# Gate matrices of a PEER layer from split operands: one 256-column product per token instead of one 128-column fp32 product

## The reference

```
q = (xb @ wq).reshape(PEER_TOKEN_BLOCK, PEER_HEADS, 2, PEER_HALF_DIM)
s = jnp.einsum('thpd,hpnd->thpn', q, keys).astype(jnp.float32)
s1, i1 = lax.top_k(s[:, :, 0], PEER_TOPK)
s2, i2 = lax.top_k(s[:, :, 1], PEER_TOPK)
...
top_s, pos = lax.top_k(cand_s, PEER_TOPK)
idx = jnp.take_along_axis(cand_i, pos, axis=-1)
gate = jax.nn.softmax(top_s, axis=-1)
act = jax.nn.gelu(jnp.einsum('thkd,td->thk', u[idx], xb).astype(jnp.float32), approximate=False)
return jnp.einsum('thk,thkd->td', (gate * act).astype(xb.dtype), v[idx])
```

## Time and profile before

| | us |
|---|---|
| median of the runs | 3306.17 |
| the profiled execution's own time | 3303.77 |
| its span | 3302.0 |
| PE busy | 3233.7 (98%) |
| DVE busy | 2537.3 (77%) |
| POOL busy | 2078.6 (63%) |
| ACT busy | 1409.5 (43%) |
| gate products on PE (1536 instructions), busy | 202.7 |

### The profile page before, as it was taken

The page is one execution under the profiler, slowest core; times in us unless marked ns, Lnnn a source line. Parts: engine busy times, 40 slices in busy tenths (PEclk is TensorE's granted clock), DMA queues, the critical chain, the costliest instruction groups (busy, mean ns, idle before and its releaser), DMA issues. The chain is left out here.

```text
span 3302.0 us, 47513 instructions
## 1 busy us (share of the span) xinstructions
PE 3233.7 (98%) x17562; PEld 2882.6 (87%) x17562; DVE 2537.3 (77%) x4630; ACT 1409.5 (43%) x2756; POOL 2078.6 (63%) x1388
## 2 busy tenths in 40 slices
PE   8999999999999999999999999999999999999998
PEld 6787789999999988888787877899999999888886
DVE  8964469876966688888877734798769656988888
ACT  2244113566666433333322531245666664333332
POOL 7913776666677655555499047766666776555553
PEclk9999999999999999999999999999999999999999
DMA  4211326688899999999622012257888999999995
GB/s 150 89 46 39 103 77 201 230 305 297 298 344 353 353 389 372 364 369 363 244 90 90 33 52 92 94 202 255 300 298 298 349 353 352 386 373 365 369 366 197
DMA packets 312918, 817.11 MB, mean 247 GB/s; under 512 B 22512, under 2 KB 119792, under 8 KB 309360
## 3 DMA queue, kind: packets, MB, share of 16 engines
q1 hardware_dynamic: 112496, 348.98, 30.7%
q0 software_dynamic: 73728, 268.47, 20.9%
q10 hardware_dynamic: 126464, 196.63, 17.0%
HBM read 712.79 MB, written 101.19 MB: 247 GB/s over the span
## 5 line engine op out<-in xcount | busy, mean ns | idle before, releaser
L1323 POOL TENSOR_TENSOR u_lo<-panel,u_hi 128x1024 fp32r<-128x1024 f32 x256 | 619.4, 2420 | 317.6 <-ACT u_hi L1122 314.4
L605 PE MATMUL ps<-hT_hi,u_lo 128*128 128x384 f32 x2048 | 700.3, 342 | 0.0
L605 PE MATMUL ps<-hT_lo,u_hi 128*128 128x384 f32 x2048 | 684.6, 334 | 0.0
L605 PE MATMUL ps<-hT_hi,u_hi 128*128 128x384 f32 x2048 | 684.6, 334 | 0.0
L605 PE MATMUL ps<-v_hi,w_lo 128*128 128x512 f32 x1536 | 598.0, 389 | 3.0 <-DVE w_lo L1907 2.9
L605 PE MATMUL ps<-v_hi,w_hi 128*128 128x512 f32 x1536 | 597.6, 389 | 0.0
L605 PE MATMUL ps<-v_lo,w_hi 128*128 128x512 f32 x1536 | 597.5, 389 | 0.0
L1340 POOL TENSOR_TENSOR v_lo<-panel,v_hi 128x1024 fp32r<-128x1024 f32 x128 | 312.8, 2444 | 370.6 <-ACT v_hi L1184 370.5
L1184 ACT CAST v_hi<-panel 128x1024 fp32r<-128x1024 f32 x256 | 269.0, 1052 | 633.0 <-PE ps L605 626.5
L1273 POOL TENSOR_TENSOR ring_hi<-panel,cst 128x512 fp32r<-128x512 f32 x244 | 283.7, 1163 | 359.4 <-PE ps L585 250.8
L1122 ACT CAST u_hi<-panel 128x1024 fp32r<-128x1024 f32 x256 | 268.1, 1048 | 446.5 <-PE ps L605 435.4
(11 more groups left out here) (272 smaller groups left out, 5695.1 us busy)
## 6 DMA issues: line engine op xcount, KB each, us to landing
panel<-in_u SPq DMA_DIRECT2D x256, 512.0 KB
panel<-in_v SPq DMA_DIRECT2D x256, 512.0 KB
gate_scratch<-arena ACTq DMA_DIRECT2D x24, 2048.0 KB
act_scratch<-arena ACTq DMA_DIRECT2D x124, 384.0 KB
arena<-act_scratch ACTq DMA_DIRECT2D x62, 768.0 KB
arena<-gate_scratch ACTq DMA_DIRECT2D x62, 768.0 KB
panel<-in_w_in SPq DMA_DIRECT2D x28, 1024.0 KB, 5.2
panel<-in_wq SPq DMA_DIRECT2D x16, 1024.0 KB, 5.1
```

The costliest lines, as they stand in the source:

```text
L605: mm = nc.tensor.matmul(o, lhs[a], rhs[b_], start=(start and n == 0), stop=(stop and n == 2))
L1323: pr.mark(nc.gpsimd.tensor_tensor(u_lo[:, j % URING].rearrange("p c n -> p (c n)"), u_tile(j), u_hi[:, j % URING].rearrange("p c n -> p (c ...
```

## The change

The gate products are done with operands of fp32r instead of fp32. The one-hots are exact in any format; the gates are split into a high part (rounded to fp32r) and a low part (the rest). For each token hot2 (now bf16) is weighed twice, by the high and by the low gate, into two halves of a 256-column operand `gated`. One matmul of hot1 by these 256 columns gives two 128x128 halves in PSUM, which are added on the way out: ACT copies the first half to `gmat` (`keep_half`), and DVE adds the second to it (`keep_gates`, now on DVE). Four tokens now take two PSUM banks, so the product of chunk k+1 waits until the sum of k is out (`g_kept` of k, before: of k-1), and there is one buffer of `gated`. DVE's `keep_gates(k-2)` stands at the head of its gate chunk k. Every 32 chunks DVE makes the high and low gates with two instructions of 128x128. The DMA of a finished block goes one chunk later, the transposes of the table go into the middle of the chunk, ACT's copy of them ahead of its wait for the chunk, and DOTS is spread anew: two dots in three chunks where the routing lies, five in four chunks from 20 to 45.

```diff
-    DOTS.append(min(DOTS[-1] + 1 + (chunk_ >= 58 and chunk_ % 2 == 0), SLOTS - LATE_DOTS))
+    routed_beside = chunk_ < 20 or 46 <= chunk_ < 60
+    DOTS.append(min(DOTS[-1] + 1 + (chunk_ >= 60 and chunk_ % 2 == 0) + (20 <= chunk_ < 46 and chunk_ % 4 == 3)
+                    - (routed_beside and chunk_ % 3 == 2), SLOTS - LATE_DOTS))
...
+            hot1 = half("hot1", 2 * CHUNK * NK)[:].rearrange("p (b c k) -> p b c k", b=2, c=CHUNK)
+            gated = half("gated", 2 * CHUNK * NK)[:].rearrange("p (c r k) -> p c r k", c=CHUNK, r=2)
...
+        hot2 = sb("hot2", [P, 2, CHUNK, NK], BF16)
...
+        chunk_banks = ps[:, GBANKS[0]:GBANKS[1] + 1, :].rearrange("p b (c r n) -> p (b c) r n", c=2, r=2)
...  (PE)
                     for c in range(NC):
+                        if j in TURNS and c == NC // 2:
+                            i = TURNS[j]
+                            pe.wait_ge(table_ready.sem, layer * table_ready.per_layer + i)
+                            if j > FIRST_CHUNK:
+                                pe.wait_ge(g_kept.sem, layer * g_kept.per_layer + j - FIRST_CHUNK)
...
-                        if k >= 2:
-                            pe.wait_ge(g_kept.sem, layer * g_kept.per_layer + k - 1)
+                        if k >= 1:
+                            pe.wait_ge(g_kept.sem, layer * g_kept.per_layer + k)
...
                         for c in range(CHUNK):
-                            mm = nc.tensor.matmul(g_bank(k)[:, c * NK:(c + 1) * NK],
-                                                  hot1[:, k % 2, c, :], hot2[:, k % 2, c, :], start=True, stop=True)
+                            mm = nc.tensor.matmul(chunk_banks[:, c].rearrange("p r n -> p (r n)"), hot1[:, k % 2, c],
+                                                  gated[:, c].rearrange("p r n -> p (r n)"),
+                                                  start=True, stop=True)
...  (ACT)
                     pr.mark(nc.scalar.copy(gmat[:, b_ % 2, :, at_:at_ + CHUNK],
-                                           g_bank(k).rearrange("p (c n) -> p n c", c=CHUNK)), g_kept)
+                                           chunk_banks[:, :, 0, :].rearrange("p c n -> p n c")), g_half)
...
-                        last = nc.scalar.activation(hot2[:, k % 2, c, :], hot2[:, k % 2, c, :], ACT.Copy,
-                                                    scale=tabT[:, 2, t:t + 1])
+                        high = gate_hi[t // P % 2][:, t % P:t % P + 1].bitcast(F32)
+                        for half, scale in enumerate((high, tabT[:, 2, t:t + 1])):
+                            last = nc.scalar.activation(gated[:, c, half], hot2[:, k % 2, c], ACT.Copy, scale=scale)
...  (DVE)
+                        step(nc.vector.tensor_copy(high[:], tabT[:, 2, toks]))
+                        nc.vector.tensor_tensor(tabT[:, 2, toks], tabT[:, 2, toks], high[:].bitcast(F32), ALU.subtract)
...
+                def keep_gates(k):
+                    b_, at_ = k // 8, k % 8 * CHUNK
+                    dve.wait_ge(g_half.sem, layer * g_half.per_layer + k + 1)
+                    kept = gmat[:, b_ % 2, :, at_:at_ + CHUNK]
+                    pr.mark(nc.vector.tensor_tensor(kept, chunk_banks[:, :, 1, :].rearrange("p c n -> p n c"), kept,
+                                                    ALU.add), g_kept)
```

More of the change, by code:

```diff
@@ L139, in build @@
         with ExitStack() as shared:
+            half("below_hots", 9600)
+            hot1 = half("hot1", 2 * CHUNK * NK)[:].rearrange("p (b c k) -> p b c k", b=2, c=CHUNK)
+            gated = half("gated", 2 * CHUNK * NK)[:].rearrange("p (c r k) -> p c r k", c=CHUNK, r=2)
+            gate_hi = [half(f"gate_hi{k}", P) for k in range(1)]
+        with ExitStack() as shared:
             half("between", 21504)
@@ L389, in build @@
         g_full = sig("g_full", NG)
+        g_half = sig("g_half", NG)
         g_kept = sig("g_kept", NG)
@@ L867, in _ @@
                     for c in range(NC):
+                        if j in TURNS and c == NC // 2:
[3 more added lines that the diff above has]
+                                pe.wait_ge(g_kept.sem, layer * g_kept.per_layer + j - FIRST_CHUNK)
+                            else:
+                                pe.wait_ge(gate_sig.sem, layer * gate_sig.per_layer + 8)
+                            for k in range(3):
+                                mm = nc.tensor.transpose(table_bank[:, k * P:(k + 1) * P], table[:, k, :], ident)
+                            pr.mark(mm, table_turned)
                         mm = matmul3(a_bank(j)[:, 0:DT], [x_[:, j % URING, c, :] for x_ in (u_hi, u_lo)],
@@ L870, in _ @@
                     pr.mark(mm, a_full)
[L871 to L880, removed]
                     if 0 <= j - FIRST_CHUNK < NG:
@@ L1212, in _ @@
                         pr.mark(nc.scalar.activation(gate_e[:], gate_e[:], ACT.Exp), sel_exp)
+                    if j in TURNS:
+                        i = TURNS[j]
+                        act.wait_ge(table_turned.sem, layer * table_turned.per_layer + i)
+                        pr.mark(nc.scalar.copy(tabT[:, :, (i - 1) * P:i * P], table_bank[:, 0:3 * P]
+                                               .rearrange("p (k t) -> p k t", k=3)), tab_ready)
                     act.wait_ge(a_full.sem, layer * a_full.per_layer + j + 1)
@@ L1218, in _ @@
                     activations(j)
-                    if j in TURNS:
-                        i = TURNS[j]
-                        act.wait_ge(table_turned.sem, layer * table_turned.per_layer + i)
-                        pr.mark(nc.scalar.copy(tabT[:, :, (i - 1) * P:i * P], table_bank[:, 0:3 * P]
-                                               .rearrange("p (k t) -> p k t", k=3)), tab_ready)
                     if 0 <= j - FIRST_CHUNK < NG:
-                        keep_gates(j - FIRST_CHUNK)
+                        keep_half(j - FIRST_CHUNK)
+                    if 8 <= j - FIRST_CHUNK <= NG and (j - FIRST_CHUNK) % 8 == 0:
+                        send_gates((j - FIRST_CHUNK) // 8 - 1)
                     if 0 <= j + 1 - FIRST_CHUNK < NG:
@@ L1824, in one_hots @@
                         dve.wait_ge(tab_ready.sem, layer * tab_ready.per_layer + k // 32 + 1)
+                        toks = slice(k * CHUNK, k * CHUNK + P)
+                        high = gate_hi[k // 32 % 2]
+                        step(nc.vector.tensor_copy(high[:], tabT[:, 2, toks]))
+                        nc.vector.tensor_tensor(tabT[:, 2, toks], tabT[:, 2, toks], high[:].bitcast(F32), ALU.subtract)
                     if k >= 2:
@@ L1870, in _ @@
                 for k in range(NG):
+                    if k >= 2:
+                        keep_gates(k - 2)
                     one_hots(k)
@@ L1882, in _ @@
                         dot(s)
-                for s in range(DOTS[NG], SLOTS - LATE_DOTS):
+                for k in (NG - 2, NG - 1):
+                    keep_gates(k)
+                    for s in range(DOTS[k + 2], DOTS[k + 3]):
+                        dot(s)
+                for s in range(DOTS[NG + 2], SLOTS - LATE_DOTS):
                     dot(s)
```

27 lines of the change are left out of this document (11 added, 16 removed).

## The result

| | before | after |
|---|---|---|
| median of the runs, us (four each, taken together) | 3306.68 | 3336.27 |
| profiled execution, us | 3303.77 | 3336.19 |
| span of that execution, us | 3302.0 | 3334.3 |
| mean granted clock | 0.995 | 0.989 |

The ratio is 1.0088, 95% interval 1.0076 to 1.0100. The forecast was 3302, its range 3272 to 3324. The result is slower, which had 0.26, and by more than rival 3 gave.

What follows compares the result with a forecast made beforehand. PE, busy 98%, was taken to bound the kernel. A layer: -40.3 PE, +18.0 ACT, +15.8 DVE, +3.0 tables, +2.2 transposes, less 0.7 of earlier stalls: -2.0. Two layers: -4, so 3302 us, range 3272 to 3324 (own range 3290 to 3312).

Steps and rivals of the forecast that it cites:

- rival 3: DVE takes the lead: its sum costs 0.9 us instead of 0.60, or dots wait longer for rows; 3319 us, chance 0.25.
- PE's block: Four gate products of 256 fp32r columns take 0.48 us instead of 0.90, making PE's chunk 4.63 us.
- ACT's chain: Eight ACTIVATEs take 2.455 us, so every second chunk without routing stalls PE; a pair takes 9.79 us, 18.0 a layer.
- the sum: DVE's 128x512 addition of the low half in each gate chunk, priced at 0.60 us.
- the moved transposes: In the middle of chunks 28 and 60 they wait for the previous chunk's gates: about 1.1 us each, 2.2 a layer.
- rival 1: ACT hides: bf16 ACTIVATEs start 0.20 us apart, removing ACT's stalls; 3268 us, chance 0.16.
- rival 2: The full gain: ACT and DVE both follow PE's shorter chunk, -81 us; 3225 us, chance 0.05.
- rival 4: The product isn't a single pass at 256 columns: 1.80 us a block, +173 us; 3479 us, chance 0.03.
- 74.8 were forecast by DVE's work: First routed stretch, 14 chunks: 38.1 us routing, 1.80 a chunk, 10 dots at 1.15; PE alone would need 64.8.
- 38.1 + 14 x 1.80 + 9 x 1.15 = 73.6: DVE's work in the second routed stretch: routing, 1.80 us a chunk, 9 dots; it makes PE wait on DVE.
- forecast as free: Chunks without routing beside them: DVE's idle time pays for its addition; 2.95 of 4.9 us with one dot.
- The exponential's chunk: Chunk where ACT loads two tables: PE's stall grows from 0.36 to 2.0 us, taken as 1.5 more, twice a layer.

Runs made afterwards that it cites:

- neither addition: Kernel after, without the low gate's ACTIVATEs (but in chunk 0 of each layer) and without DVE's sum: 3252.14 us, ratio to the kernel before 0.9833.

## Why the prediction was wrong

Right were the unit prices: PE's block at 0.48 us (4.64 a chunk with neither addition, forecast 4.63), ACT's chain with a pair of 9.76 (9.79), the sum at 0.60 from start to start, and the moved transposes, for which PE waited 0.9 us each (1.1). Rivals 1, 2 and 4 are excluded by the same rows. In rival 3 the sign was right, but its priced mechanism (a sum of 0.9 us) was not: L1853 has a mean of 690 ns, and the next instruction starts 0.60 after it. Its other half, dots that wait longer for their rows, came true at a place that it did not name, the end of the stage.

The first routed stretch took 74.98 us of PE where 74.8 were forecast by DVE's work, and that is partly luck. DVE's own way, from the one-hots of chunk 6 to those of chunk 20, took 77.8 us: three instructions met POOL's subtraction (1.77, 1.91 and 1.54 us), where before one did (1.51), and PE's stretch did not take all of it over.

Wrong were three things. The forecast was -2.0 us a layer and the result +16, a miss of 18: 7.6 of it are the start of the v stage, 6.8 the gate chunks, and 3.7 lie outside both.

1. *The second routed stretch.* The step "38.1 + 14 x 1.80 + 9 x 1.15 = 73.6" took the 38.1 us of routing from the first stretch and used it for both. By the same sum of DVE's work the routing of the second took 42.3 us in the kernel before, two holds (2.46 and 2.12 us) in it; it took 47.8 in the kernel after, and 38.2 with POOL's subtraction cut short. So the work is the same, and the term was short of the holds. Chunks 46 to 60 took 88.05 - 7.59 = 80.5 us, 6.9 more than forecast. Four small instructions in it met POOL's subtraction and took 2.0 to 2.5 us; with POOL's cut short the same 14 chunks took 75.0 (80.52 - 5.50). Before the change such holds cost PE nothing, as its rows show; now most of each is paid, since little covers DVE. The sign of it was in the earlier trace rows: L1907, taken there as a price of 1.31 us for two SBUF operands, is a mean over 0.546 to 2.870 us with a median of 0.560. The chunk ahead (45), forecast as free, took 7.59, at least 2.4 above a free one: the 2.40 us row at 851.26 lies in it, and with POOL's cut short it took 5.50.
2. *A missing term, the end of the stage.* +7.6 us a layer. The prediction priced each dot in its chunk, and put nothing for the dots that the new list takes away from there: it counted 10 and 9 dots in the routed stretches instead of 14, a gain of some 5 us each, and did not ask where the dots go. Six more of them than before went behind the last sum, where the v stage waits. This is the largest single part of the result, 15.3 of 32.3 us.
3. *The exponential's chunk* was put at a stall of 2.0 us; on PE it is 2.43. Small.

Ahead of the stage 3.8 us of the first layer are without a wait of PE in changed code. In the kernels of this study, all with the change, chunk 0 began between 619.5 and 623.2 us, with no relation to the edit that I can see, and at 617.8 in the one profile of the kernel before. The granted clock in 150 to 250 us was 1.00 before, and 0.97 or 0.98 in all thirteen kernels with the change. What lowers it is open.

## What to carry to other kernels

When a change cuts the engine that bounds, ask of every other engine how late it may now be, and look through its rows for single instructions far above their usual length: they were free only under the old slack. A count that is lowered in one place (dots, loads, copies) is raised in another, and the price is that of the other place, here the start of the next stage. Two additions on different engines that cover each other should be tried alone and together, since each alone shows less than its part.

## What the runs showed of the hardware

- A small DVE instruction on SBUF operands took up to 2.5 us while POOL subtracted 128x1024 elements, and went back to 0.2 to 0.3 us when that instruction was cut to 64 columns (0.32 us). In the kernel after, a 128x800 product with an operand in PSUM took 0.99 us 56 times of 56; without one it took 1.77 to 2.48 in eight of eight.
- fp32r products of 256 columns start 0.12 us apart (four with their share of 4.64 us: 0.48); 384 cost 0.173 and 512 0.227 here.
- Behind one DMA of 2 MB (median 11.9 us from issue to landing) dots waited 4.6 to 5.8 us for gathered rows, once in eight chunks; four of 512 KB, one a chunk, took 18 us off the whole, 12 of them in the two gate stages.
- After a wait of 8.1 us PE was granted 0.50 of its clock (1143 to 1145 us), and 512-column products started 0.43 us apart instead of 0.23 for about 3 us.
